# Rows of h2, expert numbers and the last key scores: who moves them, and when, in a one-core hybrid layer on Trainium2

## The reference

```
h2 = RMSNorm(x) * (1 + scale2(c)) + shift2(c)
q = (h2 @ wq)                        # 8 heads x 2 halves x 128
s1, s2 = q . sub_keys                # 16 lists of 128 scores per token
v1,i1 = top16(s1); v2,i2 = top16(s2)
sc,ci = top16(all 256 sums v1+v2)    # per head
e = i1[ci // 16] * 128 + i2[ci % 16] # expert numbers, 8 x 16 per token
g = softmax(sc)
x = x + gate2(c) * sum_k g_k * gelu(h2 . exp_u[e_k]) * exp_v[e_k]
out = RMSNorm(x)
```

## Time and profile before

| what | value |
|---|---|
| median of 3 runs | 846.58 us (844.03 to 846.83) |
| the profiled execution | 847.16 us, span 845.4 us |
| PE busy / PEld busy | 819.9 / 783.5 us |
| DVE, ACT, POOL busy | 560.8, 171.8, 208.6 us |
| DMA, mean over the span | 339 GB/s, 286.39 MB |
| chain that ended last | PE 86%, DMA 7%, DVE 5% |

### The profile page before, as it was taken

How to read it: one execution, slowest core, us unless ns; L and a number is a source line. 1 busy time by engine, 2 the same in 40 slices (tenths; PEclk the granted TensorE clock), 3 DMA queues, 4 the chain that set the end, 5 groups by cost and what they waited for, 6 DMA issues and landing times.

```text
span 845.4 us, 14556 instructions
## 1 busy us (share of the span) xinstructions
PE 819.9 (97%) x5758; PEld 783.5 (93%) x5758; DVE 560.8 (66%) x1134; ACT 171.8 (20%) x449; POOL 208.6 (25%) x216
## 2 busy tenths in 40 slices
PE   6999999999989999999999999999999999999996
PEld 4998879888979999999999999989999999999996
DVE  4959889698994998688788898554553344343302
ACT  4454575542111112121111111000000000000003
POOL 2000000000104321655434436533222323322100
PEclk9999999999999999999999999999999999999998
DMA  9998781653898998999999999999999999999951
GB/s 336 405 373 333 328 371 78 274 187 114 226 273 276 411 409 290 382 408 409 409 393 365 361 393 377 410 408 409 409 409 409 378 408 391 389 388 398 342 174 50
DMA packets 75909, 286.39 MB, mean 339 GB/s; under 512 B 9483, under 2 KB 11707, under 8 KB 74562
## 3 DMA queue, kind: packets, MB, share of 16 engines
q1 hardware_dynamic: 48482, 191.00, 59.1%
q0 software_dynamic: 27360, 94.47, 29.6%
HBM read 283.90 MB, written 1.52 MB: 338 GB/s over the span
## 4 chain that ended last, share of the span: by engine, by line
PE 86%; DMA 7%; DVE 5%; ACT 1%; issue 1%; ACTq 0%; SPq 0%; DVEq 0%
PE banks L1223 35%; PE banks L1194 32%; DMA raw<-in_u_t 3%; PE banks L941 3%; PE banks L1206 2%; PE banks L859 2%; PE banks L894 2%; PE banks L937 2%; DMA raw<-in_w_mod 2%; DMA raw<-in_v_b 2%; PE banks L1010 1%; PE banks L864 1%; DVE sc_w L1330 1%; PE banks L910 1%; PE banks L1242 1%
## 5 line engine op out<-in xcount | busy, mean ns | idle before, releaser
L1223 PE MATMUL banks<-act,raw 128*128 128x168 f32 x2048 | 306.1, 310 | 0.4
L1223 PEld LDWEIGHTS banks<-act,raw 128*128 128x128 f32 x2048 | 294.8, 191 | 10.4 <-DMA raw<-in_v_b 10.4
L1194 PE MATMUL banks<-hT,raw 128*128 128x168 f32 x2048 | 298.4, 307 | 3.2 <-DMA raw<-in_u_t 3.1
L1194 PEld LDWEIGHTS banks<-hT,raw 128*128 128x128 f32 x2048 | 292.3, 190 | 4.7 <-DMA raw<-in_u_t 4.7
L1696 DVE SCALAR_TENSOR_TENSOR row_sums<-rows,weight,row_sums 128x1024 f32<-128x1024 f32 x85 | 109.2, 1285 | 142.7 <-DMA rows<-in_v_b,idx 124.0
L541 POOL DMA_INDIRECT rows<-in_u_rows,idx x88 | 109.4, 1243 | 128.1 <-DVE dots L1673 91.7
L541 POOL DMA_INDIRECT rows<-in_v_b,idx x88 | 86.2, 980 | 179.7 <-PE banks L1223 142.5
L1673 DVE CUSTOM_DVE_ANT_0 rows<-rows,h_rows 128x1024 f32<-128x1024 f32 x88 | 105.9, 1221 | 18.7 <-issue 13.4
L791 ACT ACTIVATE turned<-banks,ccol 128x256 f32<-128x256 f32 x8 | 3.8, 473 | 293.6 <-PE banks L1223 293.6
L749 ACT ACTIVATE act<-banks 128x168 f32<-128x168 f32 (+20 forms) x121 | 33.1, 273 | 121.5 <-PE banks L1194 114.8
L508 POOL DMA_DIRECT2D h_lines<-h_stage x1 | 0.5, 541 | 211.4 <-ACT h_stage L774 211.4
(11 more groups left out here) (238 smaller groups left out, 825.5 us busy)
## 6 DMA issues: line engine op xcount, KB each, us to landing
raw<-in_u_t SPq DMA_DIRECT2D x128, 512.0 KB
raw<-in_v_b SPq DMA_DIRECT2D x128, 512.0 KB
wq<-in_wq SPq DMA_DIRECT2D x2, 4096.0 KB, 18.2
sh_w<-in_w_mod SPq DMA_DIRECT2D x8, 512.0 KB, 13.2
sc_w<-in_w_mod SPq DMA_DIRECT2D x8, 512.0 KB, 13.4
win<-in_w_in SPq DMA_DIRECT2D x8, 512.0 KB, 14.1
win<-in_w_in SPq DMA_DIRECT2D x1, 4096.0 KB, 20.8
sc_w<-in_w_mod SPq DMA_DIRECT2D x2, 2048.0 KB, 23.4
```

The lines of the kernel that those rows point to most:

```text
L1194: last = nc.tensor.matmul(dst, raw[n % RAW][:, c * P:(c + 1) * P], hT[:, c, 0:MANY], start=(c == 0), stop=(c == DC - 1))
L1223: return nc.tensor.matmul(chunk_place(c)[:, 0:MANY], raw[(BLOCKS + j) % RAW][:, c * P:(c + 1) * P], act[:, j, :], start=(j == 0 and c < 4) ...
```

## The change

It moves the 64-token kind's h2 rows from SBUF to SBUF in two DMAs on SP's queue, reads the other two kinds from HBM on SP's queue between blocks, writes and reads the expert numbers on SP's queue, repeats each look-up position twice so that the comparison's innermost dimension is two neighbouring values, puts block 0 ahead of the last key scores, and moves the counts and paces of gathers, dots and gates.

```diff
-EARLY = 18
+EARLY = 24
-H2_AT = 4
-EXP_AT = 50
+H2_AT = 2
+H2_FIRST = (9, 11)
+H2_LATER = (58, 61)
+EXPERTS_OUT = 25
+EXPERTS_IN = 26
+EXP_AT = 52
-TURN_AT = 55
-GATE_AT = 60
+TURN_AT = 57
+GATE_AT = 62
-PACE = 1.45
-PACE_U = 1.0
+PACE = 1.5
+PACE_U = 1.1
-        part = at("part", 13312 + 1280, [P, 2, HEADS, TOPK], F16)
+        part = at("part", 13312 + 1280, [P, 2, HK, 2], F16)
...
+        h2_in, h2_late, idx_in = (loaded[n] for n in ("sh2a", "g1b", "g1a"))
...
-            return (6, 2, 4)[(g - 2) % 3]
+            return (6, 4, 2)[(g - 2) % 3]
...
                 sp.dma_start(raw[n % RAW][:, :], u_t[n] if n < BLOCKS else v_b[n - BLOCKS]
                              ).then_inc(raw_full[n % RAW], 16)
+                if n in H2_FIRST:
+                    half = H2_FIRST.index(n) * KINDS[0]
+                    sp.wait_ge(xn_ready, TT + 3)
+                    sp.dma_start(h2_rows[0][half:half + KINDS[0], :], h2_stage[0:KINDS[0], :]).then_inc(h2_in, 16)
+                if n in H2_LATER:
+                    kind = 1 + H2_LATER.index(n)
+                    count = KINDS[kind]
+                    sp.wait_ge(h2_saved, 16)
+                    sp.dma_start(h2_rows[kind][:, :],
+                                 bass.AP(tensor=h2_lines, offset=KIND_AT[kind] * D,
+                                         ap=[[0, P // count], [D, count], [1, D]])).then_inc(h2_late, 16)
+                if n == EXPERTS_OUT:
+                    sp.wait_ge(chosen_ready, 1)
+                    sp.dma_start(expert_lines.ap(), e_u[FEW0:P, :]).then_inc(idx_in, 16)
+                if n == EXPERTS_IN:
+                    sp.wait_ge(idx_in, 16 + 16)
+                    for kind in range(len(KINDS)):
+                        sp.dma_start(idx[:, KIND_AT[kind]:KIND_AT[kind + 1]], lines_of(expert_lines, kind)
+                                     ).then_inc(idx_in, 16)
...
             pool.wait_ge(xn_ready, TT + 3)
-            pool.dma_start(h2_lines.ap(), h2_stage[0:FEW, :]).then_inc(lines_moved, 16)
-            pool.wait_ge(lines_moved, H2_SAVED)
-            for n, count in enumerate(KINDS):
-                pool.dma_start(h2_rows[n][:, :],
-                               bass.AP(tensor=h2_lines, offset=KIND_AT[n] * D, ap=[[0, P // count], [D, count], [1, D]])
-                               ).then_inc(lines_moved, 16)
...
-            pool.wait_ge(chosen_ready, 1)
-            pool.dma_start(expert_lines.ap(), e_u[FEW0:P, :]).then_inc(lines_moved, 16)
-            pool.wait_ge(lines_moved, EXPERTS_SAVED)
-            spread_lines(idx, expert_lines)
-            pool.wait_ge(lines_moved, IDX_IN)
+            pool.dma_start(h2_lines.ap(), h2_stage[0:FEW, :]).then_inc(h2_saved, 16)
+
+            pool.wait_ge(idx_in, 16 + 16 + 16 * len(KINDS))
...
-                if g == 4:
+                if g == 3:
                     pe.wait_ge(proj_out, N_IN + 2)
...
-                if g in QUAD_AFTER:
+                if g in QUAD_AFTER[:-1]:
                     key_scores(QUAD_AFTER.index(g))
...
+                if n == 0:
+                    pe.wait_ge(q_sum, LISTS // 2 - 3)
...
                 if n == H2_AT:
+                    pe.wait_ge(s_out, TT * LISTS // 4)
...
                 u_block(n)
+                if n == 0:
+                    key_scores(len(QUAD_AFTER) - 1)
...
                 if i == 0:
-                    ve.wait_ge(lines_moved, H2_IN)
+                    ve.wait_ge(h2_in, 16 + 16 * 2)
+                if i == KINDS[0]:
+                    ve.wait_ge(h2_late, 16 + 16 * len(H2_LATER))
...
-                    some_dots(min(2 - places[0] % 2, EARLY - dotted[0]))
+                    some_dots(min(2, EARLY - dotted[0]))
...
-                link(nc.vector.tensor_copy(part[:, :, :, :], part_u[:, :, :, :]))
+                link(nc.vector.tensor_copy(part[:, :, :, :], spread(part_u[:, :, :, :].rearrange("p n h k -> p n (h k)"), 3, 2)))
...
-                    place = spread(spread(place_h[:, :], 1, TOPK), 1, HEADS)
-                    link(nc.vector.tensor_tensor(hit[:, :, :, :], spread(part[:, half], 3, TOPK), place,
-                                                 ALU.is_equal))
+                    place = spread(place_h[:, :].rearrange("p (q two) -> p q two", two=2), 1, HK)
+                    link(nc.vector.tensor_tensor(hit[:, :, :, :].rearrange("p h k (q two) -> p (h k) q two", two=2),
+                                                 spread(part[:, half], 2, TOPK // 2), place, ALU.is_equal))
```

More of the change, by code:

```diff
@@ L293, in hybrid_peer_layer @@
             sem, ("second_ready", "onehot_ready", "gates_ready", "gates_used", "gates_out"))
-        lines_moved = sem("lines_moved")
+        lines_moved, h2_saved = map(sem, ("lines_moved", "h2_saved"))
         gathered = [sem(f"gathered{n}") for n in range(SLOTS)]
@@ L348, in x_place, with lines_of @@
             return 3 + c // 2 % 2, c % 2 * SEQ
-        H2_SAVED, H2_IN, EXPERTS_SAVED, IDX_IN, FEW_SAVED, FEW_IN = 16, 64, 80, 128, 144, 192
+        FEW_SAVED, FEW_IN = 16, 16 + 16 * len(KINDS)
+        def lines_of(lines, kind):
+            count = KINDS[kind]
+            return bass.AP(tensor=lines, offset=KIND_AT[kind] * HK, ap=[[count, P // count], [HK, count], [1, count]])
         QUAD_AFTER = (2, 4, 6, 7)
@@ L532, in _ @@
                     pool.wait_ge(lines_moved, FEW_SAVED)
-                    spread_lines(gate_few, gate_lines)
+                    for kind in range(len(KINDS)):
+                        pool.dma_start(gate_few[:, KIND_AT[kind]:KIND_AT[kind + 1]], lines_of(gate_lines, kind)
+                                       ).then_inc(lines_moved, 16)
                 if last_user(i) is not None:
```

## The result

The changed kernel takes 841.23 us (median of 6 runs, 839.02 to 843.74) beside 846.91 for the kernel before on the same chip: ratio 0.9937, 95% interval 0.9909 to 0.9965, 5.7 us faster. The forecast was 11.5 us faster, 835.1 us. The profiled execution took 839.3 us, its span 837.5, against 847.16 and 845.4 before.

What follows compares the result with a forecast made beforehand. PE bounds the kernel, so only its waits can be won. Terms -1.7 - 3.1 + 0.5 - 7.2 = -11.5 us against 847.2 give 835.7, corrected to a median of 835.1; own range 831.5 to 839, stated range 831 to 843.5.

Steps and rivals of the forecast that it cites:

- Key scores behind block 0: Before the last key scores: block 0 fills PE's idle time; gain 1.7 us, bounds 0 and 1.7.
- h2 rows: exp_u blocks: moving POOL's reads of three 512 KB tiles ends PE's waits; gain 3.1 us, bounds 0 and 4.7.
- A few DMA engines carry two: h2 reads before the change: a thin stream on few engines slows every block, costing PE 3.1 us.
- For both and the denser early gathers I take 0.5, bounds 0 and 4: Two later h2 tiles, behind loads 58 and 61, plus denser early gathers: cost 0.5 us, bounds 0 and 4.
- third rival: From 262 on, DMA is the bound and waits only move: 24 blocks lose 6.5 us; 848.3 us, chance 0.12.
- The place named as a sign of being wrong, blocks 50 to 65: A new exp_u wait at blocks 27 to 32 or 50 to 65 would show the forecast wrong; no size.
- Expert numbers by SP: Around blocks 25 to 27: SP waits 0 to 6.7 us, load 27 stays covered, first gather at 257 to 262.
- fourth rival: SP's wait at block 26, round trip R, starves the loads: PE loses 5.8 to 11.4 us; 853 us, chance 0.08.
- The largest piece's outermost dimension of 2: Expert numbers: this piece would hold up two engines' rings in SP's queue ahead of its blocks; no separate size.
- Paired positions: DVE's position comparisons: four save 4.3 us of DVE, bounds 0 and 4.3, all off PE's path.
- The start of exp_v: Early exp_v blocks: earlier gathers cut the 10.3 us stall to 3.1; gain 7.2 us, bounds 0 and 10.3.
- The second rival: Front won, start of exp_v not: ten gathers still burst onto a full DMA; 842.3 us, chance 0.25.

Runs made afterwards that it cites:

- the early tiles alone: The changed kernel with the two later h2 tiles read behind blocks 13 and 18 instead of 58 and 61: 839.59 us, ratio 0.9913.

## Why the prediction was right and wrong

**Key scores behind block 0: right.** Forecast 1.7; the profile shows 1.7 and the run of this part alone 1.6.

**h2 rows: the gain came, undersized, but mostly not by the cause named.** I took PE's 3.1 us of waits. PEld's figure for the stretch, 4.3, was the right price: a block that begins after a wait also lasts 2.55 instead of 2.29 us, and PE's row counts only the idle time before it. "A few DMA engines carry two" accounts for 1.4 of the 4.3 us (the run in two halves), and did not fit the share of 1.02 over all 16 engines in the earlier trace rows. The rest is slow copying with full engines, and the new half tiles from SBUF are slow as well: 7.4 and 8.1 us to landing where I wrote 0.64 to 1.0 us of DMA. That they cost nothing, as forecast, is owed to the cover of the loads around them; to that extent it was luck. It mattered, because with "few engines" as the whole cause the later tiles looked harmless.

**"For both and the denser early gathers I take 0.5, bounds 0 and 4": the step that failed.** Measured in the two profiles of the changed kernel and that without pairs: 3.1, 7.1 and 6.4 us, mean 5.5; two of the three and the mean lie beyond the upper bound (so does the 4.5 with spread exp_v gathers, which change nothing before exp_v). It has two parts. The 24 early gathers from 258.51 on, 2.556 us a pair, use up the cover of the loads (12.90 us at 295.65): 3.1, 3.9 and 2.8 us, and 0.5 in the run with 18 in the old rhythm. This is the third rival's mechanism in small, 11 blocks instead of its 24, since SP's queue was not full from the start; I had given it a price only within that rival and left it out of the sum, though the earlier trace rows had 11.46 us of 11.4 with 18 dots. The later tiles behind 58 and 61: 0 to 3.6 us, some 1.9 by moving them. I costed them at the full rate and at 259 GB/s with the cover in place, while POOL's queue, which I had pausing, had gathers again. The place named as a sign of being wrong, blocks 50 to 65, fits the second part; the first stands at blocks 40 to 50, which no sign named.

**Expert numbers by SP: right.** SP waited 1.0 us for the round trip (forecast 0 to 6.7), the first gather went at 258.51 (257 to 262), load 27 was not late, and POOL's first gather of exp_u came 6.5 us sooner. The fourth rival did not come: with a wait of 1.0 us the round trip R had no price. The largest piece's outermost dimension of 2, which the prediction holds against this step, cost nothing that can be seen either (the run with the expert numbers in halves).

**Paired positions: right.** 1238 ns instead of 2290, and no time: the kernel without them is as fast. DVE, not PE, waits at block 57 (6.3 us).

**The start of exp_v: right in the mechanism, undersized in the rest.** The counting gave a stall from exp_v block 15 on for 14 blocks, 3.9 us, and I shaded it to 3.1. It began at block 14 and lasted 17: 4.7 us, and 5.4 and 4.2 in the other profiles, 1.7 more than 3.1 on the mean. I had gather 88 released near block 124 and landed near 126. It was issued at 125, and the spacing of the rows behind it puts its landing at 128.9: later than I counted. Its row was used at 527.57, in block 131 and not before 130: DVE was at dots of exp_u until then. The second rival named a burst of ten gathers; it was there (the spread gathers take 3 to 5 us of waits away in three pairs of kernels) but beside a gain, not in its place.

**The sum again.** With 4.3 for h2's rows, 5.5 and 4.8 in the two missed terms, -11.5 - 1.2 + 5.0 + 1.7 = -6.0, which makes 840.6; measured 841.2 and 841.8. The last microsecond is of the size by which the end varies (last section).

## What to carry to other kernels

When gathers and loads share the DMA engines, add up the bytes of each stretch against the cover of the load, term by term: work that starts earlier is paid for where it now runs, and a load that already used all of its cover (11.46 of 11.4 us) is the row that says so. Release what is owed a few transfers at a time; here 4 at once instead of 10 was worth 5.2 to 5.8 us in three pairs of kernels, as much as the whole change. When a slow transfer is moved, ask what makes it slow, for it takes that along, and a new source need not cure it: behind blocks with no gathers beside them the same slow copies cost nothing, while in small pieces from SBUF beside gathers they cost 8.7 us of waits.

## What the runs showed of the hardware

While the h2 rows were copied to their places from HBM (outer step 0, the same rows read several times), all traffic together made 259 GB/s with the engines full (share 1.02), 252 with gathers beside it, and 288 behind blocks 13 and 18, where ordinary loads and gathers make 408. Splitting the tile ended the trickle of 26 packets but not this, and neither did copying from SBUF: 265 and 256 GB/s in 215 to 225 with the engines full. What these copies have in common that makes them slow, no run here shows.

The granted clock fell from 1.00 to 0.50 near the end, behind the short products of few_sums, for a time that differed from run to run. The chain prices it: L1259's 48 products and the block behind them took 7.50 and 4.68 us in the profile above, and in that of the early tiles alone:

```profile
807.83 5.26 PE banks L1259 x48
813.09 3.98 PE banks L1240 x16
```

From few_sums to the end of the span that is 29.2 us against 26.0 (27.6 before): up to 3.2 us of a run that no edit here explains, and part of why runs of one kernel differ by 5 us or more. All 14 profiles have one of three values, within 0.1 us: 26.0, 27.6 or 29.2. What decides when the clock falls was not tried.

PE also waited between 264 and 270 for ACT's gelu of a block, not for a load, in some profiles (0.8 us with spread gathers, 1.3 without pairs, 1.9 with the small pieces), after ACT had stood idle for some 4 us. Its cause is open.
